# Fourier mixer stage of a diffusion step: input tiles loaded whole, three more modulation chunks issued early, past keys and values on GpSimd's queue

## The reference, cut to what matters

```python
def _fourier(z, fw):
    B, L, _ = z.shape
    zg = z.reshape(B, L, B_GROUPS, B_GROUP_DIM).astype(jnp.float32)
    zf = jnp.fft.fft2(zg, axes=(1, 3), norm='ortho').real.astype(z.dtype)
    return jnp.einsum('blgc,gcd->blgd', zf, fw).reshape(B, L, D_B)
...
    shift1, scale1, gate1, shift2, scale2, gate2 = jnp.split(mod, 6, axis=-1)
...
        mod_lat = (jax.nn.silu(c) @ w_ada[l] + b_ada[l])[:, None, :]
        attend_lat = functools.partial(_neighbourhood_attention, kc=cache_k[:, l], vc=cache_v[:, l], rpb=rpb[l])
```

## Time and profile before

| | us |
|---|---|
| median of the runs | 3121.2 |
| the profiled execution's own time | 3121.3 |
| its span in the trace | 3119.5 |
| Fourier stage in the trace, 603.1 to 761.3 | 158.2 |
| PE busy in the stage | 64.0 |
| DVE, ACT, POOL busy in the stage | 44.5, 18.4, 24.2 |

### The profile page before, as it was taken

The page is one execution under the profiler, slowest core; times in us unless marked ns, Lnnn a source line. Parts: engine busy times, 40 slices in busy tenths (PEclk is TensorE's granted clock), DMA queues, the critical chain, the costliest instruction groups (busy, mean ns, idle before and its releaser), DMA issues. The chain is left out here.

```text
span 3119.5 us, 51637 instructions
## 1 busy us (share of the span) xinstructions
PE 2812.0 (90%) x17742; PEld 2547.9 (82%) x17742; DVE 1831.6 (59%) x3176; ACT 1277.9 (41%) x2746; POOL 404.6 (13%) x568
## 2 busy tenths in 40 slices
PE   1899999725999999799699999999999979999996
PEld 1899999624888788687599999999999978888875
DVE  4443432141998899477687787666766643443545
ACT  3111111110887888232355556555655533121121
POOL 0000000012222222122400100100000000311312
PEclk6899999867999999899899999999999989999999
DMA  7322221447664362455455555444444435243333
GB/s 250 100 82 92 92 82 68 144 162 251 135 140 94 88 136 54 138 162 192 113 196 174 172 172 197 154 148 161 147 151 153 156 129 168 81 138 117 104 126 128
DMA packets 377186, 432.54 MB, mean 139 GB/s; under 512 B 91873, under 2 KB 271921, under 8 KB 374321
## 3 DMA queue, kind: packets, MB, share of 16 engines
q1 hardware_dynamic: 358289, 420.76, 43.6%
q10 hardware_dynamic: 18720, 9.44, 1.0%
HBM read 307.92 MB, written 124.19 MB: 139 GB/s over the span
## 5 line engine op out<-in xcount | busy, mean ns | idle before, releaser
L2060 PE MATMUL fu_alpha<-fu_h,fu_w 128*128 128x384 f32 x3168 | 574.2, 335 | 17.6 <-DVE fu_h L2286 10.6
L2546 PE MATMUL fd_acc<-fd_w,fd_f 128*128 128x512 f32 x2376 | 545.8, 391 | 28.7 <-DVE fd_w L2574 19.2
L2060 PEld LDWEIGHTS fu_alpha<-fu_h,fu_w 128*128 128x128 f32 x3168 | 553.0, 188 | 20.3 <-issue 20.2
L2546 PEld LDWEIGHTS fd_acc<-fd_w,fd_f 128*128 128x128 f32 x2376 | 447.3, 189 | 127.1 <-issue 18.3
L2060 PE MATMUL fu_beta<-fu_h,fu_w 128*128 128x384 f32 x1584 | 287.3, 336 | 0.6 <-DVE fu_h L2286 0.6
L2060 PEld LDWEIGHTS fu_beta<-fu_h,fu_w 128*128 128x128 f32 x1584 | 277.1, 189 | 1.1 <-issue 1.1
L552 PE MATMUL pj_gps<-pj_ht,w_in 128*128 128x256 f32 x2160 | 268.1, 284 | 0.0
L552 PEld LDWEIGHTS pj_gps<-pj_ht,w_in 128*128 128x128 f32 x2160 | 262.7, 192 | 1.3
L2570 DVE TENSOR_TENSOR fd_f<-fd_f_stage,fd_f 128x512 fp32r<-128x512 f32 (+1 forms) x110 | 89.1, 811 | 283.9 <-ACT fd_f L2526 283.8
L2526 ACT CAST fd_f<-fd_f_stage 128x512 fp32r<-128x512 f32 (+1 forms) x110 | 63.5, 579 | 442.5 <-PE fd_acc L2546 393.9
L2260 DVE TENSOR_TENSOR fu_w<-up_w_stage,fu_w 128x512 fp32r<-128x512 f32 x264 | 181.5, 689 | 84.8 <-ACT fu_w L2124 81.9
(11 more groups left out here) (203 smaller groups left out, 4225.6 us busy)
## 6 DMA issues: line engine op xcount, KB each, us to landing
up_w_stage<-in_w_gu_dram SPq DMA_DIRECT2D x88, 512.0 KB, 4.2
fu_w_sums<-w_gu_sums SPq DMA_DIRECT2D x132, 256.0 KB, 3.3
fd_w_stage<-in_w_down_dram SPq DMA_DIRECT2D x54, 512.0 KB, 3.8
fd_f_stage<-f_t SPq DMA_DIRECT2D x88, 256.0 KB, 2.6
at_k<-k_t SPq DMA_DIRECT2D x28, 704.0 KB, 12.7
w_gu_sums<-fu_w_sums SPq DMA_DIRECT2D x66, 256.0 KB, 4.5
fo_w<-in_w_ada_dram SPq DMA_DIRECT2D x8, 2048.0 KB, 11.7
up_w_stage<-in_w_gu_dram SPq DMA_DIRECT2D x44, 256.0 KB, 4.6
```

Of the source, the lines that this page charges most:

```text
L2060: mm = pe.matmul(out, w[x][:, j, k, :], b[y][:, j, k, :], start=opens and (k, x, y) == (0, HI, HI), stop=(k, x, y) == (KH - 1, LO, HI), sk ...
L2546: mm = pe.matmul(acc[:, t, at], f[a][:, slot, t * P:(t + 1) * P], w[b][:, w_at(st, slot), at], start=is_step(st, 0) and (a, b) == (HI, HI) ...
```

## The change

Four things are edited in `fourier_phase`:

1. `load_x` loads every slot of every tile as 128 whole rows, also those of tile 0. GpSimd then waits for tile 0 and clears row 0 of its slots SET_C and PLUS, and row 0 of MINUS now holds the row that SET_C's row 0 held.
2. SP issues chunks 3, 4 and 5 of w_ada right behind the tables, chunks 6 and 7 in the loop, ahead of the stores of m = 0 and 1. The loads for the context transform move ahead of the loop.
3. GpSimd issues the loads and stores of past keys and values on its own queue, the first two at the start of the stage, and waits for their stores at its end.
4. `turn_past(0)`, `copy_past(0)` and `low_past(0)` come ahead of the transform, and those of tile m+1 behind the product of chunk 3+m. The identity is loaded early.

```diff
                 def load_x(i):
                     t = i * P
-                    p0 = 1 if i == 0 else 0
-                    sp.dma_start(x[:, i, SET_A, :], chan_dft[t:t + P, :]).then_inc(x_loaded[i], 16)
-                    sp.dma_start(x[p0:P, i, SET_C, :], chan_dft[QUARTER - 1 + t + p0:QUARTER - 1 + t + P, :]).then_inc(x_loaded[i], 16)
-                    if i == 0:
-                        sp.dma_start(x[0:1, i, SET_C, :], chan_dft[HALF_T:HALF_T + 1, :]).then_inc(x_loaded[i], 16)
...
+                    for slot, row in ((SET_A, t), (SET_C, QUARTER - 1 + t), (PLUS, 3 * QUARTER - 1 + t), (MINUS, HALF_T + t)):
+                        sp.dma_start(x[:, i, slot, :], chan_dft[row:row + P, :]).then_inc(x_loaded[i], 16)
...
-                load_past(0)
+                for c in range(SLOTS, 2 * SLOTS):
+                    load_chunk(c)
+                sp.wait_ge(f_lo, I)
+                sp.wait_ge(patched, 1)
+                sp.dma_start(ctab, dft256_in.rearrange("r (i p) m -> p r i m", p=P)).then_inc(xc_loaded, 16)
+                sp.wait_ge(mid_done, 1)
+                sp.dma_start(xc, chan_dft[T_LAT:T_ALL, :].rearrange("(i p) c -> p i c", p=P)).then_inc(xc_loaded, 16)
                 for m in range(I):
-                    load_chunk(SLOTS + m)
...
+                    if 2 * SLOTS + m < CHUNKS:
+                        load_chunk(2 * SLOTS + m)
                     store_rows(m)
-                    if m < PAST_TILES - 1:
-                        load_past(m + 1)
-                    store_past(m)
-                load_chunk(CHUNKS - 1)
...
             def _(pool):
-                pool.memset(x[0:1, 0, PLUS:MINUS + 1, :], 0.0).then_inc(zeroed, 1)
+                def load_keys(t):
+                    pool.dma_start(kc[:, :], k_rows[t]).then_inc(kc_loaded, 16)
+
+                def load_values(t):
+                    pool.dma_start(vc[:, :, :], v_rows[t]).then_inc(vc_loaded, 16)
+
+                def store_keys(t):
+                    pool.wait_ge(kc_lo, t + 1)
+                    for part_ in (HI, LO):
+                        pool.dma_start(k_t[part_, :, past(t)].rearrange("(m p) t -> p m t", p=P), kct[part_][:, :, :]).then_inc(kc_stored, 16)
+
+                past = lambda t: slice(T_ALL + t * P, T_ALL + (t + 1) * P)
+                load_keys(0)
+                load_values(0)
+                pool.wait_ge(x_loaded[0], 64)
+                for slot in (SET_C, PLUS):
+                    pool.memset(x[0:1, 0, slot, :], 0.0).then_inc(zeroed, 1)
...
+                    pool.wait_ge(vc_step, (t + 1) * VC_STEPS)
+                    pool.dma_start(v_parts[past(t), :], vparts[:, :, :, :].rearrange("p h k d -> p (h k d)")).then_inc(vc_stored, 16)
+                    if t < PAST_TILES - 1:
+                        load_values(t + 1)
+                        pool.wait_ge(kc_turned, t + 1)
+                        load_keys(t + 1)
+                    store_keys(t)
+                pool.wait_ge(kc_stored, PAST_TILES * 32)
+                pool.wait_ge(vc_stored, PAST_TILES * 16)
...
                 for c in range(SLOTS):
                     ada_product(c)
+                turn_past(0)
                 for m in range(I):
                     if m == 0:
                         pe.wait_ge(f_lo, I)
...
-                    turn_past(m)
                     ada_product(SLOTS + m)
+                    if m < I - 1:
+                        turn_past(m + 1)
```

More of the change, by code:

```diff
@@ L840, in _ @@
                         sp.dma_start(cond[:, v, :], conds[v].rearrange("(k p) -> p k", p=P)).then_inc(cond_loaded, 16)
+                sp.dma_start(ident[:, :], ident_in).then_inc(ident_loaded, 16)
                 load_biases()
@@ L885, in _, with copy_past @@
                 flat = lambda ap: ap.rearrange("p s c -> p (s c)")
+                def copy_past(t):
+                    act.wait_ge(kc_turned, t + 1)
+                    if t:
+                        act.wait_ge(kc_stored, t * 32)
+                    act.copy(kct[HI][:, :, :].bitcast(F32R), kps[:, :, :]).then_inc(kc_hi, 1)
+                copy_past(0)
                 for i in range(I):
@@ L908, in _ @@
                         act.copy(mid_out[:, :], mid[0:1, :]).then_inc(mid_copied, 1)
-                    copy_past(m)
+                    if m < I - 1:
+                        copy_past(m + 1)
                 for t in range(2):
@@ L924, in fold @@
                 def fold(i):
-                    dve.wait_ge(x_loaded[i], 80 if i == 0 else 64)
+                    dve.wait_ge(x_loaded[i], 64)
                     if i == 0:
-                        dve.wait_ge(zeroed, 1)
+                        dve.wait_ge(zeroed, 2)
                     for ri, op in ((0, ALU.add), (1, ALU.subtract)):
@@ L945, in _ @@
                     add_bias(c)
+                low_past(0)
                 fold(0)
@@ L964, in _ @@
                     dve.tensor_tensor(out[:, s, 1, :], even[:, s, :], acc[:, s, 1, :], ALU.subtract).then_inc(acc_read, 1)
-                    low_past(m)
                     add_bias(SLOTS + m)
+                    if m < I - 1:
+                        low_past(m + 1)
                 for c in range(SLOTS + I, CHUNKS):
```

14 lines of the change are left out of this document (removed).

## The result

The changed kernel takes 3070.8 us (median of 4 runs, 3068.97 to 3071.64); the kernel before, run beside it, 3122.0. The ratio is 0.9835, 95% interval 0.9818 to 0.9852. The forecast was 3073, the range 3066 to 3088. The profiled execution has a span of 3067.2 us against 3119.5.

The account below looks back on a forecast made before the run. The prediction took the Fourier stage's longest chain as the bound, held up by 127-row loads on one DMA engine and by chunk waits in the loop: 3121.3 - 26.2 - 25.2 + 3.0 = 3072.9, so 3073 us, range 3066 to 3088.

Parts of the forecast that it names:

- Part 1, the hole: Fourier stage's start: 127-row loads run on one DMA engine; whole tiles bring single rows and first transform 26.2 us earlier.
- its low end: Range's lower end, 3066 us: DVE's table parts, 2.9 us each beside GpSimd's casts, would run without that company.
- SP's issuing: Start of the stage: sixteen whole input loads at 0.70 us each take 11.3 us from about 616, not holding inputs up.
- this sign: Sign to check in SP's queue at the start: its sixteen input loads issued in about 11 us.
- Covers: Three new steps ahead of fold 0, costed at nothing, hidden by DVE's wait until 639.2; uncovered, 2 to 3 us.
- Part 2, the loop's waits: Transform loop: loading w_ada chunks early removes TensorE's waits and slow products; rounds take 9.12 us, gain 25.2 us.
- Part 3, GpSimd's queue: Past tiles' DMAs on GpSimd's list make TensorE wait for past keys in the loop; priced at 3 us.
- T: Time one DMA issue takes of GpSimd's list; unknown beforehand, taken near 1.8 us from SP's 0.55, 0.77 and 3.30.
- 6 T - 8: TensorE's wait in us for the last key tile, where T is over 1.35: nothing at 0.77, 11.8 at 3.30.
- Data: Fourier stage's DMA traffic: some 34.5 MB, 89 us at 386 GB/s; fits with little room, low rate costs 1 to 2 us.

Follow-up runs that it names:

- e1: Kernel before with only the whole 128-row loads and GpSimd's clearing of row 0 added: 3091.8 us, ratio to before 0.9907.
- e2: Changed kernel with tile 0's three loads of 127 rows and its one-row load back: 3098.1 us, ratio to before 0.9930.
- e3: Changed kernel with tile 0's old loads back, but each load of 127 rows cut into 15 and 112: 3072.7 us, ratio to before 0.9843.
- e6: Changed kernel, but GpSimd waits until all inputs are folded and split before casting past values of tile 0: 3079.5 us, ratio to before 0.9860.
- e10: Changed kernel, but GpSimd waits for the folds only before the casts of past tile 1: 3069.8 us, ratio to before 0.9829.
- e5: Kernel before with whole-tile loads and early chunks only; past tiles stay on SP's queue, turns unmoved: 3083.6 us, ratio to before 0.9873.
- e7: Changed kernel with inputs and tables loaded ahead of all w_ada chunks, products placed two per round: 3070.4 us, ratio to before 0.9838.
- e9: Changed kernel with inputs and tables loaded ahead of all chunks, products placed 2, 1, 2, 1 and 2: 3069.2 us, ratio to before 0.9822.

## Why the prediction was right, step by step

- **Part 1, the hole: right in cause, and in size partly by luck.** Predicted 26.2 us; the first transform came 27.5 us earlier in the stage, and e1, e2 and e3 show the cause. Inside it three terms missed and nearly cancelled. The first: the single rows were in at about 635.9, not 639.2. e6 has the same queue, and its DVE waits for them until 32.71 us into the stage, which is 635.94 here. The prediction put all inputs behind the three chunks and the issue of the rows on top. But by 626.18, when chunk 2's product could start, the DMA engines had moved 7.69 MB since the stage's start (22.95 us at 335 GB/s), 1.4 MB more than the chunks. GpSimd's two loads and the identity are 0.6 of it; the rest is mostly inputs that came in beside the chunks, some 0.8 MB or 2 us. The second: the folds took 3.1 us longer than before, since GpSimd cast beside them: from the single rows to the first table part 17.03 us, against 13.93 before and 13.94 in e6. The third: from the start of the first table part to the transform are 2.43 us and not 3.43, since no cast ran beside it. The prediction named faster table parts as its low end, but did not ask what the casts, now moved ahead, would do to the folds. The Trainium skill (SBUF — State Buffer, SBUF: two separate sides) describes the pair of ports as an exclusive lock. e6 and e10 agree with that so far as an operation grew by less than one of the other engine's lasts: a cast by 1.95 us beside table parts of 2.28 (e6, e10), a fold by 0.95 beside subtractions of 1.15 (e10). They can't tell a lock from another way of taking turns.
- **SP's issuing.** The prediction took 8.45 us for twelve whole loads; from 646.77 to 655.22 there are eleven, 0.77 each and not 0.70, so sixteen would be 12.3. They took 16.95, but from 610.63 on, and ended at 627.58, where the sum had about 627.3. So this sign failed as it was written, and nothing hung on it.
- **Covers.** GpSimd's wait with its clearings, and the past keys of tile 0, were put at nothing: fold 0 began at 631.31 as said. It took 4.7 us with the casts beside it, not 2.7, and the single rows just covered that: DVE came to them at 635.99.
- **Part 2, the loop's waits: the sum right, the owner wrong.** Predicted 25.2 less 3; the loop from the first transform to the stage's end went from 78.4 to 52.9, 25.5 us. The four waits were 18.0 of it, and the products behind them, which took 13.9 us together instead of 7.7, another 6.1; these ran at a lower granted clock (0.50, the 1.2 GHz level, from 711.0 to 714.7 and from 752.4 to 756.0), and the loop now runs at 1.00 (668 to 698). A round was said to take 9.12 and takes 9.01. But the prediction put the sum under the early chunks, and gave the emptier queue of SP no term of its own. e5 shows that with the chunks early and the past tiles still on SP, TensorE waits 10.2 us for keys.
- **Part 3, GpSimd's queue: too dear.** Priced at 3 us for T near 1.8; T is 0.54 to 0.77, and by the prediction's own 6 T - 8 that is no wait. None is there. The price came from leaning toward SP's longest row for another engine's issues; the median row, 0.77, was the right one. That GpSimd's DMAs would be late beside DVE's work was not seen: five issues from 634.75 on, beside the folds, took 0.55 to 0.77 us each, as in the loop, and the values issued at 635.32 were in by 641.81, as fast as SP's median before (6.6). The Trainium skill (SBUF — State Buffer, SBUF: two separate sides) names VectorE's 2-port perf-mode operations as what keeps GpSimd from writing descriptors, and not every operation on two SBUF tensors; the prediction left that condition out. The forecast did not rest on it.
- **Data.** The stage moved 34.7 MB (105.12 us at 330 GB/s), as the prediction's 34.5 says, and data sets when the chunks arrive in e7. The prediction said "fits, with little room", and so it is: an earlier transform alone won 0.7 us of stage (e7), a better order of the products 5.4 (e9).
- The forecast was 2.2 us above the median. Of the stage's 53.0 us it had 48.4; missing were the 3 us of T, 1.3 of part 1 and 0.3 of the loop, 4.6 in all. The rest of the program was 0.7 longer and the profiled execution 1.8 below the median, so a good part of the closeness is luck.

## What to carry to other kernels

Where the DMA share is near one sixteenth and an issue takes ten microseconds, look at the row count of the load just ahead of it, and cut it into counts that spread (15 and 112 did here). When loads and stores released by different engines share one in-order queue, moving one ahead only moves the wait: measure the edits together and each alone before giving the gain to one. Before bringing work forward in a stage, add up its bytes; once the DMA engines are full from end to end, an earlier start alone is worth next to nothing (0.7 us in e7).

## What the runs showed of the hardware

- A load of 127 rows runs on one DMA engine for 10 us, judged by the share of 0.07, about a sixteenth, and the rate (254 KB, 25 to 26 GB/s). It also holds SP's queue: the next issue took 9.8 to 10.2 us; as 15 and 112 rows it costs nothing that can be seen (e3).
- Where GpSimd and DVE ran side by side, both lost, and the shorter operation lost more. Beside DVE operations of 0.4 us a cast took 0.60 to 0.95 and the DVE operation up to 1.37 us (0.42 alone); beside DVE's table parts the cast took 2.56 and the table part 2.8 on average (2.28 alone).
- GpSimd's issue of a 256 KB load took 0.54 to 0.77 us and landed in 3.7 to 7.5 over the stage; SP's in the kernel before took 0.43 to 1.32 and landed in 3.1 to 9.7.
